# Splitting fp32 matmul operands with a rounding copy and one subtraction in place of mask, subtraction and copy

## The reference, cut to what matters

```python
for l in range(2):
    proj = rms_norm(x, attn_norm[l]) @ w_in[l]
    h_mla, h_diff, h_ch = jnp.split(proj, ...)
    o_mla = rms_norm(mla_attention(h_mla, ...), mla_out_norm[l])
    o_diff = diff_attention(h_diff, ...)
    o_ch = rms_norm(chunk_attention(h_ch, ...), chunk_out_norm[l])
    x = x + jnp.concatenate([o_mla, o_diff, o_ch], axis=-1) @ w_out[l]
    h = conv3(rms_norm(x, ffn_norm[l]) @ w_ffn_in[l]) + conv_b[l]   # 2 x 2816 wide, causal taps
    u, g = jnp.split(h, 2, axis=-1)
    x = x + (silu(g) * u) @ w_ffn_out[l]
x = rms_norm(x, final_norm)
z = rms_norm(x, norm_mix) @ w_in_2
q, k, v, f, u_ssm, g_attn, g_ssm = jnp.split(z, ...)
mixed = sigmoid(g_attn) * (forgetting_attention(q, k, v, f) @ w_proj_attn) \
      + sigmoid(g_ssm) * (s5_scan_gelu_glu(u_ssm) @ w_proj_ssm)
x = x + mixed @ w_out_2
x = x + moe(rms_norm(x, norm_ffn))          # top group of 4, top 2 of its 8 experts
```

## Time and profile before

| | us |
|---|---|
| median of 3 runs | 2090.63 (2089.95 to 2091.28) |
| span of the profiled execution | 2087.8 |
| median minus that span | 2.8 |
| PE busy | 1905.3 (91%) |
| DVE busy | 1278.3 (61%) |
| ACT busy | 748.9 (36%) |
| POOL busy | 776.3 (37%) |

### The profile page before, as it was taken

How to read it: one execution, slowest core, us unless ns; L and a number is a source line. 1 busy time by engine, 2 the same in 40 slices (tenths; PEclk the granted TensorE clock), 3 DMA queues, 4 the chain that set the end, 5 groups by cost and what they waited for, 6 DMA issues and landing times.

```text
span 2087.8 us, 26051 instructions
## 1 busy us (share of the span) xinstructions
PE 1905.3 (91%) x8932; PEld 1344.2 (64%) x8933; DVE 1278.3 (61%) x2070; ACT 748.9 (36%) x1273; POOL 776.3 (37%) x1231
## 2 busy tenths in 40 slices
PE   7998899999999998988999999889999889697784
PEld 5873467888887785456888888666766567333232
DVE  7566667668844637567667864689974885311013
ACT  4256734334422336653334432321225442110000
POOL 0425766676500003676666630065632020111110
PEclk9999999999999999999999999999999998799897
DMA  4210122322233321112323322233322162699995
GB/s 163 91 64 21 61 91 101 111 102 100 96 111 109 127 70 49 41 66 96 111 102 110 105 96 96 108 111 129 105 79 82 41 253 114 234 366 425 421 367 203
DMA packets 42554, 278.11 MB, mean 133 GB/s; under 512 B 7186, under 2 KB 7570, under 8 KB 20560
## 3 DMA queue, kind: packets, MB, share of 16 engines
q1 hardware_dynamic: 31248, 237.66, 30.6%
q0 software_dynamic: 10192, 27.50, 3.6%
q10 hardware_dynamic: 1008, 11.53, 1.4%
HBM read 262.29 MB, written 23.69 MB: 137 GB/s over the span
## 4 chain that ended last, share of the span: by engine, by line
PE 77%; DVE 10%; DMA 7%; ACT 4%; issue 2%; POOL 0%; SPq 0%; ACTq 0%; POOLq 0%; DVEq 0%
PE bank L934 11%; PE bank L935 11%; PE bank L936 11%; DMA all_slots<-in_experts 4%; PE bank L1147 4%; PE bank L1149 4%; PE bank L1148 4%; PE bank L1423 3%; PE bank L1069 2%; PE bank L1083 2%; PE bank L1178 2%; PE bank L1179 2%; PE bank L1180 2%; PE bank L1426 1%; PE bank L1044 1%
## 5 line engine op out<-in xcount | busy, mean ns | idle before, releaser
L934 PE MATMUL bank<-h_high,w_high 128*128 128x512 f32 x1040 | 408.7, 393 | 18.9 <-ACT h_high L1798 12.5
L935 PE MATMUL bank<-h_low,w_high 128*128 128x512 f32 x1040 | 405.9, 390 | 0.0
L936 PE MATMUL bank<-h_high,w_low 128*128 128x512 f32 x1040 | 405.9, 390 | 0.0
L1686 ACT ACTIVATE w_high<-extra 128x2048 fp32r<-128x2048 f32 (+2 forms) x97 | 169.6, 1750 | 284.9 <-DVE w_low L2193 284.8
L2190 DVE TENSOR_SCALAR extra<-ring 128x2048 int32<-128x2048 int32 (+2 forms) x97 | 112.2, 1156 | 211.2 <-PE bank L936 114.8
L934 PEld LDWEIGHTS bank<-h_high,w_high 128*128 128x128 f32 x1040 | 196.0, 188 | 69.3 <-ACT w_high L1686 14.1
L936 PEld LDWEIGHTS bank<-h_high,w_low 128*128 128x128 f32 x1040 | 196.0, 188 | 41.2
L935 PEld LDWEIGHTS bank<-h_low,w_high 128*128 128x128 f32 x1040 | 196.1, 189 | 40.4 <-issue 0.2
L2193 DVE TENSOR_TENSOR w_low<-ring,extra 128x2048 fp32r<-128x2048 f32 (+2 forms) x97 | 204.4, 2107 | 3.3
L1148 PE MATMUL bank<-act_low,w_high 128*128 128x512 f32 x264 | 102.9, 390 | 0.0
L1815 ACT ACTIVATE work<-bank,par 128x512 f32<-128x512 f32 x88 | 66.2, 772 | 76.7 <-PE bank L936 76.7
(11 more groups left out here) (584 smaller groups left out, 4091.8 us busy)
## 6 DMA issues: line engine op xcount, KB each, us to landing
all_slots<-in_experts SPq DMA_DIRECT2D x29, 2048.0 KB, 18.2
ring<-in_w_ffn_in SPq DMA_DIRECT2D x44, 1024.0 KB, 4.9
all_slots<-in_experts SPq DMA_DIRECT2D x30, 1024.0 KB, 24.0
ring<-in_w_ffn_out SPq DMA_DIRECT2D x32, 704.0 KB, 4.1
ring<-in_w_feature SPq DMA_DIRECT2D x14, 1024.0 KB, 4.8
ring<-in_w_rest SPq DMA_DIRECT2D x9, 1024.0 KB, 4.9
ring<-in_w_out SPq DMA_DIRECT2D x8, 1024.0 KB, 4.9
powers_d<-work POOLq DMA_DIRECT2D x16, 512.0 KB, 3.4
```

Source lines behind the costliest of these rows:

```text
L934: pe.matmul(dst, high[:, at], h_high[:, k, :], start=p == 0, stop=False)
L935: pe.matmul(dst, high[:, at], h_low[:, k, :], start=False, stop=False)
L936: return pe.matmul(dst, low[:, at], h_high[:, k, :], start=False, stop=p == KD - 1)
L1686: act.activation(w_high[par_][:, lo:words], w_part[par_][:, lo:words], ACT.Copy).then_inc(w_split, 1)
```

## The change

The masks go. ACT copies the original block or tile into the high part, and this copy rounds to `fp32r`. It waits for the data itself (`arrived` for weights, `normed`, `out_normed`, `ffn_act`, `glued`, `mixed` for activations) and, where the high buffer may still be in use, for PE. DVE then subtracts the high part from the original, and PE waits for that subtraction (`w_split`, `h_split`, `act_split`). The semaphores `*_masked` and `*_lowered` are replaced by `*_rounded`.

```diff
-    def split_high(n, par_, words=SLOT, lo=0):
-        act.wait_ge(w_lowered, n + (l * SPLITS + 1))
-        act.activation(w_high[par_][:, lo:words], w_part[par_][:, lo:words], ACT.Copy).then_inc(w_split, 1)
+    def round_weights(n, par_, words=SLOT, lo=0, at=l):
+        act.wait_ge(arrived[n % RING], at * (LAYER_BLOCKS // RING * 16) + 16 * (n // RING + 1))
+        act.activation(w_high[par_][:, lo:words], ring[n % RING][:, lo:words], ACT.Copy).then_inc(w_rounded, 1)
...
-    def mask_and_lower(slot, par_, words, count, lo=0):
-        dve.tensor_scalar(w_part[par_][:, lo:words].bitcast(I32), ring[slot][:, lo:words].bitcast(I32), HIGH_BITS,
-                          None, ALU.bitwise_and).then_inc(w_masked, 1)
-        dve.wait_ge(w_masked, count)
-        dve.tensor_tensor(w_low[slot][:, lo:words], ring[slot][:, lo:words], w_part[par_][:, lo:words],
-                          ALU.subtract).then_inc(w_lowered, 1)
+    def lower(slot, par_, words, count, lo=0):
+        dve.wait_ge(w_rounded, count)
+        dve.tensor_tensor(w_low[slot][:, lo:words], ring[slot][:, lo:words], w_high[par_][:, lo:words],
+                          ALU.subtract).then_inc(w_split, 1)
...
-    for k in range(KD + 1):
+    for k in range(KD + 2):                       # normalise_and_split
         if k < KD:
             dve.scalar_tensor_tensor(h[:, k, :], x[:, k, :], gain(k), rstd[:, 1, :], ALU.mult, ALU.mult).then_inc(normed, 1)
-        if k > PLAIN:
-            dve.wait_ge(normed, l * (2 * KD) + (norm * KD + k))
-            split_tile(i, k - 1 - PLAIN)
+        if k > PLAIN + 1:
+            lower_tile(i, k - 2 - PLAIN)
```

The subtraction of a tile now follows the norm by two tiles instead of one. The blocks 0 and 1 of the output weights are copied on ACT after attention blocks 48 and 52 and subtracted on DVE one block later:

```diff
+OUT_WEIGHTS_AT = (FIRST_MLA + 8, FIRST_MLA + 12)
...
+                    elif t in OUT_WEIGHTS_AT:                                   # ACT, after the exponential of block t
+                        round_weights(BLOCK_OUT + OUT_WEIGHTS_AT.index(t), OUT_WEIGHTS_AT.index(t))
...
+                    elif t - 1 in OUT_WEIGHTS_AT:                               # DVE
+                        lower_w_out(OUT_WEIGHTS_AT.index(t - 1))
...
-                split_high(BLOCKS_PROJ, 0)                                      # ACT, between the norm's steps
...
-                split_high(BLOCKS_PROJ + 1, 1)
...
-                split_w_out(0)                                                  # DVE, ahead of the norm's scaling
-                split_w_out(1)
```

More of the change, by code:

```diff
@@ L444, in build @@
         dist = extra[:, (6 + EXTRA_PROBS) * T:]
-        w_part = [extra[:, 6 * T + n * SLOT:6 * T + (n + 1) * SLOT] for n in range(2)]
         h_high = second_names(("before_h_high", [P, H_HIGH_AT * T], F32), ("h_high", [P, KD, T], F32R))[1]
@@ L531, in build @@
         y5 = [rstd[:, 0, :], rt_tiles[1]]
-        h2_part = work[:, 0:KD * T].rearrange("p (k t) -> p k t", k=KD)
-        mid_part = [work[:, KD * T + n * SLOT:KD * T + (n + 1) * SLOT] for n in range(2)]
         qk_place = extra[:, 0:8 * T].rearrange("p (c t) -> p c t", c=8)
@@ L1826, in conv_g @@
                     return par[:, bass.ds(j + lo, 1)]
-                split_high(SPLIT_FFN + 1, 1)
                 for p, k in enumerate(TILE_ORDER[2]):
-                    act.wait_ge(h_lowered, l * (3 * KD) + (2 * KD + p + 1))
-                    act.activation(h_high[:, k, :], h_part[:, k, :], ACT.Copy).then_inc(h_split, 1)
-                for j in range(2):
-                    conv_tap(j, j, done(l, "ffn_in", j, 0), None)
-                    split_high(SPLIT_FFN + j + 2, j)
-                    silu(j, l * (2 * JF) + 2 * (j + 1))
@@ L1836, in _ @@
-                with act.Fori(1, LOOPED // 2) as r:
-                    for s in range(2):
-                        j = r * 2 + s
-                        conv_tap(j, s, r * 4 + (done(l, "ffn_in", s, 0)), r * 2 + (l * JF + (s - 1)))
-                        split_high(j + (SPLIT_FFN + 2), s)
-                        silu(s, r * 4 + (l * (2 * JF) + 2 * (s + 1)))
+                    act.wait_ge(normed, l * (2 * KD) + (KD + k + 1))
+                    act.activation(h_high[:, k, :], h[:, k, :], ACT.Copy).then_inc(h_rounded, 1)
@@ L1842, in _, with round_acts @@
                 words = block_words(BLOCK_FFN_OUT)
-                def act_high_parts(lo, hi):
+                def round_acts(lo, hi):
                     for n in range(lo, hi):
-                        act.wait_ge(act_lowered, l * JF + (n + 1))
-                        act.activation(act_high[n], act_part[n], ACT.Copy).then_inc(act_split, 1)
-                for j in range(LOOPED, JF - 2):
-                    conv_tap(j, j % 2, done(l, "ffn_in", j, 0), l * JF + (j - 1))
-                    split_high(SPLIT_FFN + j + 2, j % 2)
+                        act.wait_ge(ffn_act, l * JF + (n + 1))
+                        act.activation(act_high[n], act_ff[:, n, :], ACT.Copy).then_inc(act_rounded, 1)
@@ L1852, in _ @@
+                for j in range(JF - 2):
+                    conv_tap(j, j % 2, done(l, "ffn_in", j, 0), l * JF + (j - 1) if j >= 2 else None)
+                    round_weights(BLOCK_FFN_IN + j + 2, j % 2)
                     silu(j % 2, l * (2 * JF) + 2 * (j + 1))
-                    act_high_parts(2 * (j - LOOPED), 2 * (j - LOOPED) + 2)
+                    if j >= LOOPED:
+                        round_acts(2 * (j - LOOPED), 2 * (j - LOOPED) + 2)
                 conv_tap(JF - 2, 0, done(l, "ffn_in", JF - 2, 0), l * JF + (JF - 3))
-                split_high(SPLIT_OUT, 0, words)
+                round_weights(BLOCK_FFN_OUT, 0, words)
@@ L1899, in mid_weights @@
             def mid_weights(b):
-                act.wait_ge(w_lowered, MID_SPLIT + b)
-                act.activation(mid_high[b % 2][:], mid_part[b % 2], ACT.Copy).then_inc(w_split, 1)
+                n = B2_MID + b
+                if b >= 2:
+                    act.wait_ge(pe_done, done2(*MID_TILES[2 * b - 3]))
+                act.wait_ge(arrived[n % RING], RING0 + 16 * (n // RING + 1))
+                act.activation(mid_high[b % 2][:], ring[n % RING][:], ACT.Copy).then_inc(w_rounded, 1)
             def gelu_sigmoid(a_):
@@ L2037, in _ @@
             for k in range(KD):
-                tile_high2(MIXED_SPLIT + k + 1, mixed_both[:, KD + k, :], gates[:, KD + k, :])
-                if k == 2:
+                act.wait_ge(mixed, k + 1)
+                act.activation(mixed_both[:, KD + k, :], gates[:, k, :], ACT.Copy).then_inc(h_rounded, 1)
+                if k == 3:
                     weight_high2(4)
@@ L2212, in normalise_and_split, with lower_proj, lower_tile @@
+                def lower_proj(n, l=l):
+                    lower(n % RING, n % 2, block_words(n), l * SPLITS + (n + 1), PLAIN * 2 * P if n == 0 and l < LAYERS else 0)
+                def lower_tile(i, p):
+                    k = TILE_ORDER[i][p]
+                    dve.wait_ge(h_rounded, l * (3 * KD) + (i * KD + p + 1))
+                    dve.tensor_tensor(h_low[:, k, :], h[:, k, :], h_high[:, k, :], ALU.subtract).then_inc(h_split, 1)
                 def normalise_and_split(norm, i, gain):
@@ L2551, in _ @@
             dve.wait_ge(final_step, 2)
-            for k in range(KD + 1):
+            for k in range(KD + 2):
                 if k < KD:
```

281 lines of the change are left out of this document (116 added, 165 removed).

## The result

| | before | after |
|---|---|---|
| median of 15 runs each, us | 2091.17 (2089.29 to 2096.03) | 2095.76 (2093.90 to 2100.59) |
| span of the profiled execution | 2087.8 | 2093.1 |

The ratio is 1.0020, with a 95% interval of 1.0013 to 1.0028: about 4.6 us slower, at the bound of what this measurement tells from no change. The forecast was 2081, its range 2074 to 2090. The sign was wrong.

A forecast was written before the change was run, and what follows sets the result against it. The prediction took PE to bound most of the kernel (busy 91% of the span), so only PE's waits could be won. Its terms summed to -9.7 us, from 2090.6 to 2081, range 2074 to 2090.

The forecast's parts named there:

- a delay of 4 us on either engine is filled from work that is ready; I count 0.25 each: Two output-weight blocks per layer inside attention: nearly hidden, +1.0 us in all; bounds nothing and 16.9.
- rival 4: Insertions in attention are exposed, 16.9 us in place of 1.0: slower, 2097; chance 0.05.
- 0 for the second attention and its projections: Second attention: +0.5 us for a copy between exponentials, about -0.5 for a dropped mask; bounds -1 and +1.5.
- rival 2: No measurable change, about 2090: chain heads 0.7 us late, nothing behind closes up, DVE's in-order queue holds norms; chance 0.16.
- -3.2 at the output projection: Attention to output projection, twice: PE starts 1.6 us earlier each; bounds 1.1 and 1.9 each.
- Rival 1: More gain, about 2075: starts after less idle stay at 2.4 GHz, 1.8 us twice, plus far bounds; chance 0.14.
- the paragraph on prices: Full split falls from 5.45 to 4.22 us, but DVE is free 0.7 later if idle while ACT copies.
- rival 3: Feed-forward loop's ACT-DVE ping-pong becomes the bound: 0.5 us overrun on 44 blocks gives 2103; chance 0.07.
- The end of the feed-forward part: Feed-forward to its output projection: waits for `w_high` vanish, -0.9 us; bounds 0 and -0.9.
- The starts of the feed-forward part: Norm 0.5 us late but tiles lose masks: -2.3 in layer 0, -2.0 in layer 1, -4.3 in all.
- the starts of the layers: Late block against dropped masks: +0.2 us in layer 0, -0.7 in layer 1, -0.5 in all; bounds -2 to +1.4.
- The start of the second part: Eight tiles without masks end sooner, part given back in the scan's chain: -1.8 us; bounds -0.3 to -2.5.

The follow-up runs named there:

- act_only: Changed kernel with the output-weight copies left inside attention on ACT, their DVE subtractions moved behind the last head; one execution, 2093.48 us.
- back2: Changed kernel with both output-weight blocks split after the last head: copies ahead of and behind the norm's squares, subtractions ahead of its scaling; 2089.17 us, ratio 0.9986.
- move_alone: Kernel before, old split, with only the two output-weight blocks moved into attention (mask and subtraction on DVE, copy one block later); 2099.83 us, ratio 1.0036.
- spread: Changed kernel with the two output-weight insertions in attention 14 blocks apart instead of 4; one execution, 2097.07 us.
- lag3: Changed kernel with DVE subtracting the two output-weight blocks three attention blocks behind their copy instead of one; 2098.46 us, ratio 1.0024.
- pattn: Changed kernel with weight block 4 of the second part subtracted behind the sixth tile of the attention's projection instead of the fourth; 2091.62 us, ratio 0.9993.
- best: Changed kernel with `back2`, `norm_first` and `pattn` together, plus a later copy and subtraction in the second attention and a misplaced early-wait try; 2079.35 us, ratio 0.9939.
- warm5: `best2` plus five unread matmuls on PE per layer in the idle time ahead of the output projection; 2072.99 us, ratio 0.9905.
- best2: `best` with the last projection weights' subtraction in attention at block 6 instead of 4, behind the norm of compressed queries and keys; 2076.01 us, ratio 0.9916.
- norm_first: Changed kernel with weight block 1 subtracted behind the norm's tiles instead of ahead, at all four norm starts; 2091.29 us, ratio 0.9993.

## Why the prediction was wrong

**The step that failed most** is an overlap: "a delay of 4 us on either engine is filled from work that is ready; I count 0.25 each". The sum has +1.0 for it; it measured +6.9, 41% of the far bound of 16.9, by the mechanism of rival 4. What the step left out is the copy of a turn on ACT. PE soon needs it, and it stands in ACT's queue behind whatever is put in: behind an exponential that waits for DVE at the first block, right behind the weights' copy at the second. `act_only` separates the two, `back2` gets all of it back, and `move_alone` shows that the old split pays there too. `spread` costs no less behind two other blocks.

The row was on the table: PE had 0.79 us idle in 35, and I read DVE's 18 and ACT's 9 us of idle as room. What these two waited for in the same 35 us of before (line, releaser, us in total, times, longest):

```profile
DVE extra L2335 <- PE bank L1044: 4.2, 6, 1.2
...
DVE stat L2303 <- ACT extra L1765: 2.7, 3, 1.5
...
ACT x L1754 <- PE bank L1069: 5.1, 8, 1.3
ACT work L1754 <- PE bank L1069: 4.5, 10, 1.0
```

All of ACT's waits are for PE, and three quarters of DVE's (12.3 of 16.2 us); they come in pieces of at most 1.3 and 1.5 us. They stood idle mostly because PE, busy for 98%, set the pace. A copy of 1.9 us and a subtraction of 2.3 are longer than any of these pieces. Whether shorter steps would have fitted, no run shows.

My first explanation was not enough: `lag3` took the wait for the copy away, and the cost stayed.

**The second: 0 for the second attention and its projections**, which measured +3.4. The prediction had named the mechanism, DVE running its queue in order with norms held behind a subtraction, in rival 2, and then left this place out. `pattn` settles 2.4 of it; the remainder went with the later copy in `best`, which was not run alone.

**The third: -3.2 at the output projection.** The start came 1.5 us earlier, as worked out (1.6). What was missing is that PE begins there at 1.2 GHz either way, and that an earlier start bought time at the lower clock: 5.7 us of it instead of 3.6 gave 1.0 of 1.5 back in layer 0, and 0.7 in layer 1. Rival 1 had the clock on the other side, as a gain. `warm5` shows the price of the clock there: 2.9 and 2.4 us.

**The fourth: the copy ahead of the subtraction early in attention**, +1.8, was nowhere in the sum, though the paragraph on prices says that DVE is free 0.7 later where it can do nothing else. The measured 0.9 each is of that kind: ACT comes to the copy only behind an exponential (122.61), so DVE waits 1.51 where the mask took 0.68. The Trainium skill's rule in "ScalarE: Activation LUTs", "Rules for kernel authors", which the prediction set aside, has the sign right at this place; the page gives its factor of about three for bf16, not for fp32. But `best2` leaves the copy on ACT and moves only the subtraction, and the 0.9 is gone: what costs is the order.

**Right.** The loop of the feed-forward part: 0, with PE at 250.00 of 250; rival 3 did not come. The end of the feed-forward part: the right sign, -2.1 for a forecast of -0.9, and the waits for `w_high` gone. The starts of the feed-forward part: -3.4 for -4.3, the late block 0.5 as said, the tiles closer together. What went missing in layer 1 (2.0 forecast, 0.95 measured) went to the plain matmuls at the lower clock, 6.14 against 4.54 us. So did the starts of the layers, +1.4 for a forecast of -0.5: their plain matmuls took 1.3 and 1.0 us more. The start of the second part gave -1.1 for -1.8, within its bounds. The signs named for a right forecast all came (DVE down by 216 us, the idle at 4.71, the waits of the feed-forward start gone, the loop at 100%), and it was wrong all the same: none of them looks at attention.

**The base.** With attention at its forecast of +1.0 the kernel would still not have reached 2081: `back2`, which has nothing there, ran 2089.17. Part of what is missing goes with the clock. These are runs of both kernels by their mean granted clock (before: the 64 runs beside the experiments; its 15 runs of the first table have no clock on record):

```
mean clock   before: runs, median us   after: runs, median us
0.964                                  1, 2100.59
0.965        18, 2095.36               10, 2095.73
0.966         6, 2094.43                4, 2096.14
0.967         8, 2092.04
0.968         7, 2091.42
0.969        24, 2090.03
0.970         1, 2089.42
```

The kernel before has executions that last 2095 us and others that last 2090, and the clock sorts them. The profile on which the prediction rests is of the second kind (2087.8 at 0.969). The kernel after runs at 0.964 to 0.966 in all 15 runs, and at 0.965 the two kernels are 0.4 us apart. In the two profiles, 3.8 us more at the four norm starts and 1.7 at the two projections make 5.5 at the lower clock, and the span grew by 5.3; the waits added (+12.1: 6.9, 3.4, 1.8) and the waits removed are about even.

That does not make the clock a cause apart from the change. Part of the lower clock is the change's own: the stretch at 0.50 in the last projections comes behind the new wait and goes with it (`pattn`). Elsewhere the kernel's order alone does not decide it: at the start of layer 1 `best` and `best2` have the same code and the same idle time of 2.39 us, and the eight plain matmuls took 5.37 us in one and 3.67 in the other. Why all runs of after lie at 0.964 to 0.966, and those of before anywhere from 0.965 to 0.970, stays open: no execution of before at 0.965 was profiled.

## What to carry to other kernels

When work is put between the steps of a stage, ask whether the engine that sets the end has slack there and what it needs from behind the new work, not whether the others have idle time in total: theirs was waiting for that engine, in short pieces. An in-order wait costs by what is queued behind it: 3.17 us cost nothing ahead of a norm that wasn't due, 1.5 us cost 0.9 in attention, so put the half that waits behind the step that others need. As first written the change lost 4.6 us; with a few subtractions and copies elsewhere the kernel is 17 us faster than before (`best2`, 0.9916). No run has these orders with the old split, so how much of the 17 is the new split's is not shown.

## What the runs showed of the hardware

- PE begins the output projection at a granted clock of 0.50 after an idle time of 6.22, of 4.71 and of 5.10 us alike; with 0.81 us of idle it began at 1.00 (`warm5`).
- Eight plain matmuls after 2.3 to 4.3 us of idle were busy for between 3.67 and 6.70 us (before, after, `norm_first`, `best`, `best2`). At the start of layer 1, after the same idle time of 2.39, it was 3.67 in before and in `best2` and 5.37 in `norm_first` and in `best`, whose code there is that of `best2`: 1.7 us at one start of one profile need not come from the edit.
- The mean granted clock of an execution, 0.965 or 0.969, goes with 5.3 us of this kernel's time; differences below that need many runs or the clock beside each run.
